# Six query, key and value products of one attention layer as seven block products each

## The reference, cut to what matters

```python
for i in range(DEPTH):
    y = _mixer(x, positions, rel_bias_table, w_in[i], ...)
    x = _layernorm(DEEPNORM_ALPHA * x + y, ln_mix_g[i], ln_mix_b[i])
    f = _swiglu(x, ...) if i % 2 == 0 else _moe(x, router_w[j], ...)
    e = jax.nn.sigmoid(x @ w_ple_gate[i]) * (p[i] @ w_ple_proj[i])
    x = _layernorm(DEEPNORM_ALPHA * x + f + e, ln_ffn_g[i], ln_ffn_b[i])
```

## Time and profile before

| | us |
|---|---|
| median of 3 runs | 3237.35 |
| lowest and highest | 3237.31, 3238.67 |
| span of the profiled execution | 3237.5 |
| TensorE busy in it | 3185.4 (98%) |
| VectorE busy | 1049.5 (32%) |
| ScalarE busy | 409.6 (13%) |

### The profile page before, as it was taken

One profiled execution on the slowest core, in us unless ns is written; L12 is line 12 of the kernel. 1 busy time (PEld: TensorE's weight loads), 2 busy tenths in 40 slices (PEclk: granted clock), 3 DMA queues, 4 the chain that ended last, 5 costly groups with the idle time before them and its releaser, 6 DMA issues.

```text
span 3237.5 us, 76009 instructions
## 1 busy us (share of the span) xinstructions
PE 3185.4 (98%) x34760; PEld 2616.3 (81%) x34760; DVE 1049.5 (32%) x2232; ACT 409.6 (13%) x1027; POOL 50.5 (2%) x86
## 2 busy tenths in 40 slices
PE   9999999999999999999998999999999999999999
PEld 6685985777699999999997967588895976688894
DVE  2252564043201101111013661211566562210465
ACT  1240000042111000000001001210100001110100
POOL 0000000000000000000000000000000000000000
PEclk9999999999999999999998999999999999999999
DMA  7423444323699999999996444334444444434442
GB/s 255 151 98 154 182 159 172 144 107 124 240 392 358 360 418 385 426 427 426 427 426 252 172 160 171 130 130 156 157 164 162 181 150 171 155 111 149 157 177 90
DMA packets 63091, 714.11 MB, mean 221 GB/s; under 512 B 7568, under 2 KB 9232, under 8 KB 11888
## 3 DMA queue, kind: packets, MB, share of 16 engines
q1 hardware_dynamic: 59328, 703.62, 55.6%
q0 software_dynamic: 1008, 5.94, 0.5%
q10 hardware_dynamic: 2624, 2.65, 0.4%
HBM read 709.30 MB, written 1.05 MB: 219 GB/s over the span
## 4 chain that ended last, share of the span: by engine, by line
PE 94%; DMA 3%; DVE 1%; ACT 1%; issue 0%; POOL 0%; SPq 0%; POOLq 0%; DVEq 0%; ACTq 0%
PE psum L599 50%; PE psum L790 15%; PE psum L720 10%; PE psum L800 7%; PE psum L855 5%; DMA weight_ring<-in_experts 3%; PE psum L819 1%; PE psum L1152 1%; PE psum L765 1%; PE psum L637 1%; PE psum L633 1%; PE psum L886 1%; PE psum L632 0%; POOL statistics L521 0%; PE psum L1126 0%
## 5 line engine op out<-in xcount | busy, mean ns | idle before, releaser
L599 PE MATMUL psum<-arena,weight_ring 128*128 128x256 f32 (+1 forms) x5408 | 974.3, 339 | 7.6 <-DVE arena L2071 3.8
L599 PEld LDWEIGHTS psum<-arena,weight_ring 128*128 128x128 f32 x5408 | 869.5, 191 | 98.1 <-issue 14.3
L790 PE MATMUL psum<-arena,weight_ring 128*64 128x80 f32 (+2 forms) x14336 | 565.5, 237 | 7.9 <-issue 3.3
L790 PEld LDWEIGHTS psum<-arena,weight_ring 128*64 128x64 f32 x14336 | 542.8, 137 | 17.4 <-issue 9.0
L599 PE MATMUL psum<-weight_ring,arena 128*128 128x128 f32 (+3 forms) x3024 | 511.2, 326 | 2.0 <-DVE arena L1841 2.0
L599 PEld LDWEIGHTS psum<-weight_ring,arena 128*128 128x128 f32 x3024 | 385.9, 192 | 113.9 <-issue 106.8
L800 PE MATMUL psum<-arena,weight_ring 128*64 128x80 f32 (+2 forms) x7168 | 300.1, 237 | 3.0 <-issue 3.0
L1729 DVE TENSOR_TENSOR arena<-arena,psum 128x80 f32<-128x80 f32 (+2 forms) x224 | 54.5, 243 | 716.3 <-ACT arena L1319 716.3
L800 PEld LDWEIGHTS psum<-arena,weight_ring 128*64 128x64 f32 x7168 | 280.4, 137 | 3.6 <-issue 3.6
L855 PE MATMUL psum<-weight_ring,arena 128*128 128x512 f32 x384 | 168.6, 597 | 0.0
L1319 ACT ACTIVATE arena<-psum 128x80 f32<-128x80 f32 (+2 forms) x224 | 54.4, 243 | 744.3 <-PE psum L790 744.3
(11 more groups left out here) (265 smaller groups left out, 1999.4 us busy)
## 6 DMA issues: line engine op xcount, KB each, us to landing
weight_ring<-in_experts SPq DMA_DIRECT2D x224, 1536.0 KB, 12.0
weight_ring<-in_ffn_up SPq DMA_DIRECT2D x44, 2048.0 KB, 7.8
weight_ring<-in_second_wide SPq DMA_DIRECT2D x42, 2048.0 KB, 7.7
weight_ring<-in_first_wide SPq DMA_DIRECT2D x35, 2048.0 KB, 8.8
weight_ring<-in_ffn_down SPq DMA_DIRECT2D x20, 2048.0 KB, 7.7
weight_ring<-in_dense_up SPq DMA_DIRECT2D x11, 2048.0 KB, 7.8
weight_ring<-in_dense_down SPq DMA_DIRECT2D x5, 2048.0 KB, 7.8
weight_ring<-in_ffn_down SPq DMA_DIRECT2D x4, 1024.0 KB, 5.0
```

The costliest lines, as they stand in the source:

```text
L599: m = pe.matmul(o, lhs, rhs, start=i == 0, stop=i == len(terms) - 1)
L790: mm = pe.matmul(psum[g * STRIP:(g + 1) * STRIP, q % 4, m * CAP:m * CAP + tokens], w[:, m, k, g * STRIP:(g + 1) * STRIP], chosen[:, k, 0:t ...
```

## The change

Each of the six products in layer 2 of block 1 is split two by two: the 1024 model dimensions into a low and a high half, the output columns into first and second blocks, the tokens into first and second half. VectorE makes four sums of the token blocks once (`sum_qkv_tokens`) and four sums of weight blocks for each product (`sum_qkv_weights`), TensorE makes seven block products in two jobs (`name`, four of them, and `name_end`, three), ScalarE copies the first block product to SBUF and VectorE merges them with seven operations (`merge_qkv`). The job list of this layer gets six jobs more, so all later jobs of the layer change their pair of banks by two. Before the experts TensorE also waits for both sigmoids of the layer (`ple_sig`). Layer 1 keeps its products.

```diff
+QKV_SEVENS = order("dq0", "dq1", "dk0", "dk1", "dv0", "dv1")
-    (("dq0", "dq1", "dk0", "dk1"), ("route", "rank", "ple_gate1")))]
+    (halves_of(*QKV_SEVENS), ("route", "rank", "ple_gate1")))]
+QKV_FREED = {part: 7 * n + count for name, n in QKV_SEVENS.items() for part, count in ((name, 3), (f"{name}_end", 7))}
+        def qkv_weights(name, j):
+            n = QKV_SEVENS[name]
+            return extra[2 * (n % 2) + j // 2][:, j % 2 * GEMM // 4:(j % 2 + 1) * GEMM // 4]
...
+                def qkv_products(name, w, by_rows):
...
+                    for half, terms in ((name, ((of_weights(0, 0), of_tokens(0, 0)), (of_weights(0, 1), of_tokens(1, 0)),
+                                                (of_sums(1), of_token_sums(1)), (of_sums(2), of_token_sums(2)))),
+                                        (f"{name}_end", ((of_sums(0), of_token_sums(0)), (of_sums(3), of_tokens(1, 1)),
+                                                         (of_weights(1, 1), of_token_sums(3))))):
+                        if J[half] >= 4:
+                            pe.wait_ge(*banks_free(half, l))
+                        for j, (weight, token) in enumerate(terms):
+                            if half == name and j == 2:
+                                pe.wait_ge(*qkv["summed"].by(0, 4 * QKV_SEVENS[name] + 8))
+                            for m in range(1 if by_rows else 2):
+                                at = j * SEQ + m * P
+                                if by_rows:
+                                    mm = product([(pair(J, half)[:, at:at + SEQ], token(k), weight(m, k)) for k in range(KT // 2)])
+                                else:
+                                    mm = product([(pair(J, half)[:, at:at + P], weight(m, k), token(k)) for k in range(KT // 2)])
+                        mm.then_inc(f["full"].sem, 1)
...
                     pe.wait_ge(*once["slotted"].by(0))
+                    pe.wait_ge(*f["ple_sig"].by(l))
                     most = pe.value_load(busiest[0:1, 0:1], min_val=0, max_val=SEQ)
...
+                if l == 1:
+                    for name, n in QKV_SEVENS.items():
+                        act.wait_ge(*f["full"].by(l, J[name] + 1))
+                        if n:
+                            act.wait_ge(*qkv["merged"].by(0, 7 * (n - 1) + 2))
+                        nc.scalar.copy(qkv_terms[:, 3], pair(J, name)[:, 0:SEQ]).then_inc(f["qkv_copied"].sem, 1)
+                    act.wait_ge(*qkv_merged("dv1"))
...
+                def sum_qkv_weights(name):
...
+                    dve.wait_ge(*landed(c, 0))
+                    if n > 1:
+                        dve.wait_ge(*f["full"].by(l, J[f"{list(QKV_SEVENS)[n - 2]}_end"] + 1))
+                    v.tensor_tensor(o(0), of(0, 1), of(1, 1), ALU.add).then_inc(qkv["summed"].sem, 1)
+                    v.tensor_tensor(o(2), of(0, 0), of(0, 1), ALU.subtract).then_inc(qkv["summed"].sem, 1)
+                    dve.wait_ge(*qkv["summed"].by(0, 4 * n + 5))
+                    v.tensor_tensor(o(1), o(0), of(0, 0), ALU.subtract).then_inc(qkv["summed"].sem, 1)
+                    dve.wait_ge(*qkv["summed"].by(0, 4 * n + 7))
+                    v.tensor_tensor(o(3), of(1, 0), o(1), ALU.subtract).then_inc(qkv["summed"].sem, 1)
+                def merge_qkv(name):
...
+                    dve.wait_ge(*f["qkv_copied"].by(l, n + 1))
+                    if n:
+                        dve.wait_ge(*qkv["merged"].by(0, 7 * n))
+                    v.tensor_tensor(u2, first, start[:, 2], ALU.add).then_inc(qkv["merged"].sem, 1)
+                    merged_part(first, start[:, 1], 0, 0)
+                    dve.wait_ge(*qkv["merged"].by(0, 7 * n + 1))
+                    v.tensor_tensor(u3, u2, start[:, 3], ALU.add).then_inc(qkv["merged"].sem, 1)
+                    dve.wait_ge(*f["full"].by(l, J[f"{name}_end"] + 1))
+                    v.tensor_tensor(u4, u2, end[:, 0], ALU.add).then_inc(qkv["merged"].sem, 1)
+                    dve.wait_ge(*qkv["merged"].by(0, 7 * n + 3))
+                    merged_part(u3, end[:, 0], 1, 1)
+                    merged_part(u3, end[:, 2], 1, 0, ALU.subtract)
+                    dve.wait_ge(*qkv["merged"].by(0, 7 * n + 4))
+                    merged_part(u4, end[:, 1], 0, 1)
+                if l == 1:
+                    sum_qkv_tokens()
+                    sum_qkv_weights("dq0")
+                    sum_qkv_weights("dq1")
                 dve.wait_ge(*f["latent_rs"].by(l))
...
+                else:
+                    names = list(QKV_SEVENS)
+                    for n, name in enumerate(names):
+                        merge_qkv(name)
+                        if n + 2 < len(names):
+                            sum_qkv_weights(names[n + 2])
                 dve.wait_ge(*f["full"].by(l, J["cq_turn"] + 1))
```

More of the change, by code:

```diff
@@ L130, with halves_of @@
 GATES1 = spread(1, 1, 1, 1, 1, 1, 1, 1, 1, 2, 2, 2, 1, 0, 0)
+QKV_SEVENS = order("dq0", "dq1", "dk0", "dk1", "dv0", "dv1")
+def halves_of(*names):
+    return [part for name in names for part in (name, f"{name}_end")]
 JOBS1 = [order(
-    "latent0", "latent1", *with_bias, "dv0", "dv1",
+    "latent0", "latent1", *with_bias,
     "cq_turn", "ckv_turn", "uq0", "uq1", "ukv0", "ukv1", "q_turn0", "q_turn1", "k_turn0", "k_turn1",
@@ L136 @@
     "ple_proj0", "ple_proj1", "x_turn1", "ple_gate0", *last) for with_bias, last in (
-    (("dq0", "bias0", "dq1", "bias1", "dk0", "bias2", "dk1", "bias3"), ("ple_gate1", "end_turn0", "end_turn1")),
-    (("dq0", "dq1", "dk0", "dk1"), ("route", "rank", "ple_gate1")))]
+    (("dq0", "bias0", "dq1", "bias1", "dk0", "bias2", "dk1", "bias3", "dv0", "dv1"), ("ple_gate1", "end_turn0", "end_turn1")),
+    (halves_of(*QKV_SEVENS), ("route", "rank", "ple_gate1")))]
 JOBS2 = order(
@@ L151 @@
 FREED1 = dict(
-    latent0=("latent", 1), latent1=("latent", 2), dq0=("dq", 1), dq1=("dq", 2), dk0=("dk", 1), dk1=("dk", 2),
-    **{f"bias{i}": ("bias_rows", i + 1) for i in range(BIAS_JOBS)}, dv0=("dv", 1), dv1=("dv", 2), cq_turn=("cqT", 3), ckv_turn=("ckvT", 2), uq0=("q_rows", 1), uq1=("q_rows", 2),
+    latent0=("latent", 1), latent1=("latent", 2), dq0=("qkv_copied", 1), dq1=("qkv_copied", 2), dk0=("qkv_copied", 3), dk1=("qkv_copied", 4),
+    **{f"bias{i}": ("bias_rows", i + 1) for i in range(BIAS_JOBS)}, dv0=("qkv_copied", 5), dv1=("qkv_copied", 6), cq_turn=("cqT", 3), ckv_turn=("ckvT", 2), uq0=("q_rows", 1), uq1=("q_rows", 2),
     ukv0=("kv_rows", 2), ukv1=("kv_rows", 4), q_turn0=("qT", 1), q_turn1=("qT", 2), k_turn0=("kT", 1), k_turn1=("kT", 2),
@@ L366, in build @@
                     o_stats=8, o_aggr=8, o_rs=2, o_n=8, yc=2, ycT=8, gate=24, m_tmp=4, mT=6, mix=2)
+        qkv = Signals(new, "qkv_", summed=4 + 4 * len(QKV_SEVENS), merged=7 * len(QKV_SEVENS))
         moe = Signals(new, "expert_", hidden=EXPERT_UNITS, silu=EXPERT_UNITS, gated=EXPERT_UNITS, taken=4)
@@ L873, in banks_free, with of_weights, part, of_sums @@
                 def banks_free(name, l):
-                    signal, count = FREED1[list(J)[J[name] - 4]]
+                    earlier = list(J)[J[name] - 4]
+                    if l == 1 and earlier in QKV_FREED:
+                        return qkv["merged"].by(0, QKV_FREED[earlier])
+                    signal, count = FREED1[earlier]
                     return f[signal].by(l, count)
+                def qkv_products(name, w, by_rows):
+                    def of_weights(i, kk):
+                        def part(m, k):
+                            at = 2 * P * i if by_rows else (2 * m + i) * P
+                            return w[:, kk * KT // 2 + k, at:at + (2 * P if by_rows else P)]
+                        return part
+                    def of_sums(j):
+                        def part(m, k):
+                            at = 2 * P * k if by_rows else (2 * k + m) * P
+                            return qkv_weights(name, j)[:, at:at + (2 * P if by_rows else P)]
+                        return part
+                    def of_tokens(kk, h):
+                        return lambda k: xT[:, kk * KT // 2 + k, h * P:(h + 1) * P]
+                    def of_token_sums(j):
+                        return lambda k: qkv_tokens[:, j, k, :]
+                    for half, terms in ((name, ((of_weights(0, 0), of_tokens(0, 0)), (of_weights(0, 1), of_tokens(1, 0)),
[14 more added lines that the diff above has]
+                        mm.then_inc(f["full"].sem, 1)
@@ L909, in _ @@
                     w = slot(c, KT, 512)
-                    (rows(J, name, w, KT, 512) if name[:2] == "dv" else columns(J, name, w, KT)).then_inc(f["full"].sem, 1)
+                    if l == 1:
+                        qkv_products(name, w, name[:2] == "dv")
+                    else:
+                        (rows(J, name, w, KT, 512) if name[:2] == "dv" else columns(J, name, w, KT)).then_inc(f["full"].sem, 1)
                     end_unit()
@@ L1364, in _ @@
                         nc.scalar.activation(trig[:, q], angle[:, 3 + q], ACT.Sin).then_inc(once["trig"].sem, 1)
```

(28 more changed lines are left out.)

34 lines of the change are left out of this document (30 added, 4 removed).

## The result

The changed kernel takes 3230.22 us (median of 9 runs, 3227.2 to 3234.46) where the kernel before, measured beside it, takes 3238.4 (3237.31 to 3239.75): ratio 0.9976, 95% interval 0.9967 to 0.9985. That is -8.2 us where -5.3 was forecast. The time is inside the range, but the difference is not: the range was -7.9 to -0.8 us around a kernel before of 3237.35, and that kernel took 1.05 us more this time. The middle of the ratio is on the side of "faster" by over 0.2%, which had 0.28, but its interval reaches across that bound. The profiled executions have spans of 3237.5 and 3229.5 us, -8.0.

A forecast was written before the change was run, and what follows sets the result against it. TensorE, busy 98% of the span, was taken as the bound. Products -8.50, uq0 +0.67 and gather +2.53 summed to -5.3 us from 3237.35, forecast 3232.1 us; range -7.9 to -0.8 us, 3229.4 to 3236.5.

The forecast's parts named there:

- "faster" by over 0.2%: Whole kernel: measured faster by more than 0.2% (6.5 us); chance 0.28, 0.18 from Rival 1 and 0.10 the forecast's own.
- The products: Six query, key and value products on TensorE: seven block products each save 5.20 plus 3.30 us, together 8.50 us.
- Neither end (7.8 or 10.3): Saving on the six products: 7.8 us if value products gained only 1.30 each, 10.3 if small pieces were equally efficient.
- VectorE in time: VectorE's sums and merges during the products: 7.0 us per 12.5 us period, so TensorE never waits; cost nothing.
- uq0: Start of uq0 after the products: cq_turn's scaling stands behind dv1's merge, so uq0 starts 0.67 us later; ends 0 and 1.3.
- The gather: Before the experts: sigmoid wait ahead of count read and branch starts the gather 2.53 us later; ends 1.13 and 4.70.
- Rival 1: Before the gather: TensorE's read and branch take at most a few tenths of a us; 3230 to 3231 us; chance 0.27.
- goes through in full: Behind the gather: any TensorE shift before the DMA's unbroken run from 1264 us reaches the kernel's end whole.
- Rival 2: At the branch ahead of the gather: an uncovered instruction fetch gap of 1.2 to 1.8 us; 3233.5 us; chance 0.13.
- Rival 3: Pause before the gather: clock falls, gather and first expert run half speed some 4 us, losing 2; 3234 us; chance 0.14.
- Rival 4: Same pause: clock falls for about 17 us, TensorE loses 7 us; 3239.1 us; chance 0.06.

The follow-up runs named there:

- doubled sums: Changed kernel with VectorE making the first of its four weight sums of each product four times more; 3229.49 us, one run.
- eight more sums: Changed kernel with VectorE making the first of its four weight sums of each product eight times more; 3261.79 us, one run.
- wait behind the branch: Changed kernel with TensorE's sigmoid wait moved behind the read of the busiest expert's count and the branch; median 3228.84 us, ratio 0.9973.
- wide values: Changed kernel with both value products undone, again 16 matmuls of 512 columns each; queries and keys keep seven block products; median 3233.53 us, ratio 0.9983.
- exchanged pairs: Changed kernel with PSUM pairs of the router's job and ple_gate1 swapped, sigmoid wait gone; medians 3229.41 and 3226.49 us, 3228.2 over 12 runs.

## Why the prediction was right, and where it was not

- The products: -8.50 worked out, -8.51 measured. The 128-column row came from the dense network, the 256-column one from this stage's own queries and keys, and both carried over to 0.01 us a product. Neither end (7.8 or 10.3) came.
- VectorE in time: right where it mattered, with dk0's sums ready at 577.2. The first weights had landed earlier than the 551.3 worked out: dq0's sums began right behind the token sums and were ready at 554.1 instead of 556.0. The slack was shown from both sides.
- uq0: +0.67 worked out, +0.66 measured.
- The gather: 2.53 worked out, 2.28 measured. VectorE's 1.40 us for read and branch was close to TensorE's 1.10. Rival 1 (a read of a few tenths) was wrong.
- Those three give -5.57 us, so the sum held for what it added up. The measured -8.2 is 2.6 more, and this is not the scatter of one trace, although single runs of the changed kernel spread over 7 us. All 51 runs of the kernel before in the four comparisons have a median of 3238.5, all 16 of the changed kernel 3230.1. That is -8.4 us, and drawing again from these runs gives a 95% interval of some -9.4 to -7.0, which leaves out -5.57. The step of the prediction that missed it is that a shift "goes through in full": everything behind the gather, and the clock ahead of it, was taken to stay as it was.
- What differed there, in traces. From latent1 to the end of the experts the kernel before took 1192.4 and 1190.8 us. The changed kernel's matmuls took 1183.5, 1182.6 and 1183.7 (the third with doubled sums). The means are 8.3 apart: 5.6 of the three terms, 1.1 of the clock behind the router (it fell in both traces of the kernel before and in one of the three others, for 1.7 us each time), 1.5 of the experts and 0.1 of the rest. In the first pair it was -1.69, -1.64 and, in the next network, +0.98. Five traces can't tell whether the clock falls less often in the changed kernel.
- The experts' 1.5 us stay open. From gather to the end of the experts the traces took 883.1 and 881.6 us before. With the sigmoid's wait it was 881.5, 880.8 and 880.2 (changed kernel twice, doubled sums), 882.4 (eight more sums), 882.1 (wait behind the branch) and 881.9 (wide values, its slow gather included). With exchanged pairs it was 879.8, 880.0, 879.8, 880.0 and 880.6. What TensorE's idle time shows in the first pair, before and then after (total us, times, longest):

```profile
PE psum L790 <- issue: 3.3, 3, 1.8
PE psum L800 <- issue: 3.0, 3, 1.2
PE psum L790 <- DMA weight_ring<-in_experts: 2.0, 9, 0.4
```

```profile
PE psum L821 <- issue: 4.3, 4, 2.0
PE psum L811 <- DMA weight_ring<-in_experts: 2.6, 12, 0.4
```

With 2.7 us for ScalarE in both, that is 11.0 us before and 9.6 after, so 1.4 of the 1.64 us are shorter waits, and those are shorter "issue" gaps. Over the other traces the same sum mostly goes with the stage's time (10.6 us before again, 11.1 with eight more sums, 8.8 to 9.7 with exchanged pairs; 7.6 with wide values doesn't fit). But the gaps alone came to 4.3 and to 6.1 us in two traces of the changed kernel. What sets their length, and how much of it belongs to the change, nothing here tells.
- Luck: the time is inside the range only because the kernel before ran 1.05 us above the 3237.35 that the sum started from. And 3230.2 is the time of rival 1 (3230 to 3231), whose cheap read did not happen.
- Rival 2 (a fetch gap at the branch): no trace had one there; the pause was 2.21, 2.21, 2.21, 2.24 and 2.30 us. Rival 3 happened once, for 1.4 us. Rival 4 (a long fall) did not happen.

## What to carry to other kernels

A product of an fp32 block by seven instead of eight wins what rows of the narrower matmul in the same kernel say, here 9.4% of a product with 128 columns and 12% with 256 rather than 12.5%, as long as VectorE's sums and merges fit into one product's time. What it loses is at the edges: the last merge stands in front of the next stage, and shifted PSUM pairs can bring a new wait. A register read behind such a wait costs twice (here 1.11 us of wait and 1.10 us of read and branch), since read and branch lose their cover; give the buffer another pair, or put the wait behind the branch.

A sum of such terms is worth no more than the stages that it leaves out: here they moved by 2.8 us, a third of the whole. So list the stretches with a granted clock under 1 in the trace before costing an edit, and set the medians of many runs beside the sum.

## What the runs showed that I had not expected

A block of 16 small matmuls (8 moving columns, 3.6 us, TensorE 100% busy by the profile) was followed by a granted clock of 0.50 in 8 of 12 traces, for 1.7 to 1.8 us lost in six of them and 3.4 in two. In three of the eight the block itself already took longer (3.79, 4.49 and 4.61 us). The busy row doesn't show it; the clock column and the weight loads do, 0.34 us each instead of 0.19. The Trainium skill, "TensorE: Matmul & The Clock Gate", section "HAM oscillation", speaks of idle gaps; here the fall came with no idle at all.
